# Differential attention with the query projection two heads ahead and the key projection one

## What is computed

```
q, k, v = jnp.split(h @ w_in, [2 * H * dk, 4 * H * dk], axis=-1)
q = apply_rope(...); k = apply_rope(...)        # 2 halves of 64 per head
s = jnp.einsum('bqhcd,bkhcd->bhcqk', qi, k) * scale
p = masked_softmax(s, key_pos[None, :] <= qpos[:, None])
a = p[:, :, 0] - lam * p[:, :, 1]               # the difference of two softmaxes
o = jnp.einsum('bhqk,bkhd->bqhd', a, v)
o = rms_norm(o, subln_g) * (1.0 - lambda_init)
return o.reshape(B, S, H * dv) @ w_out
```

## Time and profile before

| | us |
|---|---|
| median of 3 runs (1627.14 to 1628.72) | 1627.54 |
| the profiled execution | 1626.89 |
| its span, as the hardware profiler has it | 1625.1 |
| TensorE busy | 1511.1 (93%) |
| VectorE busy | 815.0 (50%) |
| ScalarE busy | 711.6 (44%) |
| GpSimd busy | 577.1 (36%) |

### The profile page before, as it was taken

One profiled execution on the slowest core, in us unless ns is written; L12 is line 12 of the kernel. 1 busy time (PEld: TensorE's weight loads), 2 busy tenths in 40 slices (PEclk: granted clock), 3 DMA queues, 4 the chain that ended last, 5 costly groups with the idle time before them and its releaser, 6 DMA issues. The chain is left out here.

```text
span 1625.1 us, 22951 instructions
## 1 busy us (share of the span) xinstructions
PE 1511.1 (93%) x7566; PEld 1246.5 (77%) x7566; DVE 815.0 (50%) x1233; ACT 711.6 (44%) x1245; POOL 577.1 (36%) x343
## 2 busy tenths in 40 slices
PE   6898887999999999999889898989999999999988
PEld 5766655888888888778778787878788888888877
DVE  5666665365455410155556777676364554420053
ACT  5243433454444422247436364636364444432252
POOL 3524534344454444333310101010244444444332
PEclk9988987999999999999899999999999999999999
DMA  4311010132322322232410101010133223222222
GB/s 172 122 34 53 26 52 26 66 130 90 102 91 91 102 101 94 78 119 78 158 41 14 40 14 39 13 39 13 52 117 102 92 90 103 95 99 91 91 88 81
DMA packets 35336, 125.96 MB, mean 78 GB/s; under 512 B 4304, under 2 KB 5072, under 8 KB 35024
## 3 DMA queue, kind: packets, MB, share of 16 engines
q1 hardware_dynamic: 31824, 115.88, 21.0%
q10 hardware_dynamic: 3456, 9.33, 1.6%
HBM read 123.09 MB, written 2.10 MB: 77 GB/s over the span
## 5 line engine op out<-in xcount | busy, mean ns | idle before, releaser
L291 POOL TENSOR_TENSOR w_lo<-w_raw,w_hi 128x1024 fp32r<-128x1024 f32 x213 | 528.4, 2483 | 918.6 <-ACT w_hi L360 918.5
L1173 PE MATMUL banks_a<-nT_hi,w_hi 128*128 128x512 f32 (+1 forms) x936 | 356.5, 381 | 3.3 <-DVE nT_lo L759 3.0
L360 ACT ACTIVATE w_hi<-w_raw 128x1024 fp32r<-128x1024 f32 x213 | 225.6, 1061 | 305.6 <-PE banks_b L1182 128.1
L1173 PE MATMUL banks_a<-nT_lo,w_hi 128*128 128x512 f32 (+1 forms) x936 | 354.0, 378 | 0.0
L1173 PE MATMUL banks_a<-nT_hi,w_lo 128*128 128x512 f32 (+1 forms) x936 | 353.5, 378 | 0.0
L1173 PEld LDWEIGHTS banks_a<-nT_hi,w_hi 128*128 128x128 f32 x936 | 180.3, 193 | 35.6 <-DVE nT_lo L759 3.9
L1173 PEld LDWEIGHTS banks_a<-nT_lo,w_hi 128*128 128x128 f32 x936 | 179.8, 192 | 31.0
L1173 PEld LDWEIGHTS banks_a<-nT_hi,w_lo 128*128 128x128 f32 x936 | 179.4, 192 | 31.4
L434 ACT ACTIVATE y<-banks_a,conv 128x512 f32<-128x512 f32 x88 | 68.7, 780 | 203.9 <-PE banks_a L1173 203.4
L809 DVE SCALAR_TENSOR_TENSOR y<-banks_a,conv,y 128x511 f32<-128x511 f32 x88 | 66.0, 750 | 177.8 <-ACT y L434 177.3
L908 DVE TENSOR_REDUCE nm<-banks_b 128x2 f32<-128x256 f32 (+2 forms) x96 | 79.1, 824 | 59.5 <-PE banks_b L1332 39.4
(11 more groups left out here) (260 smaller groups left out, 2613.3 us busy)
## 6 DMA issues: line engine op xcount, KB each, us to landing
w_raw<-in_w SPq DMA_DIRECT2D x213, 512.0 KB, 3.2
g_pre<-in_gains ACTq DMA_DIRECT2D x6, 512.0 KB, 3.7
x<-in_x SPq DMA_DIRECT2D x4, 512.0 KB, 9.5
g_post<-in_gains ACTq DMA_DIRECT2D x4, 512.0 KB, 5.1
out<-x SPq DMA_DIRECT2D x4, 512.0 KB, 2.7
pe_raw<-in_pT ACTq DMA_DIRECT2D x2, 512.0 KB, 4.4
w1k<-in_w ACTq DMA_DIRECT2D x1, 1024.0 KB, 4.9
w1v<-in_w ACTq DMA_DIRECT2D x1, 1024.0 KB, 6.8
```

The source lines that it names most:

```text
L291: pool.tensor_tensor(w_lo[slot][:, :], w_raw[k % RAW][:, :], w_hi[slot][:, :].bitcast(F32), ALU.subtract).then_inc(S["w_lo_done"], 1)
L360: act.activation(w_hi[u % RING][:, :], w_raw[u % RAW][:, :], ACT.Copy).then_inc(S["w_hi_done"], 1)
L1173: m = pe.matmul(bank[:, cols], w[:, k * P:(k + 1) * P], r[:, k, cols], start=(k, pas) == (0, 0), stop=(k, pas) == (KT - 1, 2))
```

## The change

The queries are now projected two heads ahead and the keys one head ahead. The weight units are used in the same order as before: keys of h + 1, then queries of h + 2.

- TensorE projects, within head h, the keys of h + 1 first (between the first scores and the second values) and then the queries of h + 2. The queries of head 1 are projected before head 0. The six parts of a head stand at the same six places as before, only part 3 and what follows hold queries; head 6 has keys only, head 7 nothing.
- VectorE ropes the keys of h + 1 between mixes 2 and 3, and does `query_half(h + 2)` at the end of the head. `o_variance` moves ahead of the third maximum, and the fourth maximum ahead of mix 2.
- ScalarE does the fourth pair of exponentials before the third `pT`, moves the first `w_high` of a head behind that `pT`, and the second behind the last `pT`. Three instead of two `w_high` of queries and keys are made before head 0.
- GpSimd does one `low`, then the query rope, then `o_normed`, then the other `low`.
- The loops cover heads 1 to 4; heads 5 to 7 are written out.

The scores themselves are the same instructions.

```diff
--- before.py
+++ after.py
@@ -331,11 +331,11 @@
             lows(0, ahead)
             with chain.loop(0, (DIFF_HEADS - 2) // 2, 2 * (4 * NEWTON + 1)) as i:
                 for p in range(2):
+                    u = ahead + 2 * p
+                    low(u, u % RING, u + 4 * i + 1)
+                    query_rope(2 * i + (p + 2), p)
                     o_normed(2 * i + p)
-                    query_rope(2 * i + (p + 2), p)
-                    for k in range(2):
-                        u = ahead + 2 * p + k
-                        low(u, u % RING, u + 4 * i + 1)
+                    low(u + 1, (u + 1) % RING, u + 4 * i + 2)
             o_normed(DIFF_HEADS - 2)
             o_normed(DIFF_HEADS - 1)
             lows(ahead + 2 * (DIFF_HEADS - 2), UNITS)
@@ -562,7 +562,8 @@
                 signal(act.activation(oT0_hi[:, bass.ds(h, 1), :].rearrange("p a n -> p (a n)"), A[2][:, :],
                                       ACT.Identity, scale=subg[:, :]), "oThi_done", h + 1)
 
-            def head(h, p, first=False, last=False, i=0, per=0, u=0):
+            def head(h, p, first=False, keys=True, queries=True, i=0, per=0, u=0):
+
                 exps(h, p, 0)
                 exps(h, p, 1)
                 if not first:
@@ -570,25 +571,26 @@
                 p_turned(h, 0)
                 exps(h, p, 2)
                 p_turned(h, 1)
-                if not last:
+                exps(h, p, 3)
+                p_turned(h, 2)
+                if keys:
                     w_high(u, i, per)
-                p_turned(h, 2)
-                exps(h, p, 3)
                 if not first:
                     oT_high(h - 1)
-                if not last:
+                p_turned(h, 3)
+                if queries:
                     w_high(u + 1, i, per)
-                p_turned(h, 3)
 
             UH = PLAN["qk"] + RING
-            w_high(UH)
-            w_high(UH + 1)
+            for u in range(3):
+                w_high(UH + u)
             act.wait_ge(S["lam_ready"], 1)
-            head(0, 0, first=True, u=UH + 2)
-            with chain.loop(0, (DIFF_HEADS - 2) // 2, 2) as i:
+            head(0, 0, first=True, u=UH + 3)
+            with chain.loop(0, (DIFF_HEADS - 4) // 2, 2) as i:
                 for p in range(2):
-                    head(2 * i + (p + 1), (p + 1) % 2, i=i, per=4, u=UH + 4 + 2 * p)
-            head(DIFF_HEADS - 1, 1, last=True)
+                    head(2 * i + (p + 1), (p + 1) % 2, i=i, per=4, u=UH + 5 + 2 * p)
+            for h in range(DIFF_HEADS - 3, DIFF_HEADS):
+                head(h, h % 2, keys=h < DIFF_HEADS - 1, queries=h < DIFF_HEADS - 2, u=UH + 3 + 2 * h)
             o_out(DIFF_HEADS - 1)
             w_high(PLAN["out0"] + RING)
             oT_high(DIFF_HEADS - 1)
@@ -955,33 +957,34 @@
                 rope(A[k], (qT, kT)[k][p][:, :], ("qrope_done", "krope_done")[k], h + 1,
                      tmp=(sh[:, :], t1[:, :], t2[:, :]), scale=(1.0, SCALE)[k])
 
-            def head(h, p, first=False, last=False):
+            def head(h, p, first=False, keys=True, queries=True):
+
                 maxima(0, 0, "scores_done", "negmax_done", 4 * h)
                 maxima(1, 2, "scores_done", "negmax_done", 4 * h + 1)
                 mix(h, p, 0)
                 mix(h, p, 1)
-                maxima(2, 0, "scores_done", "negmax_done", 4 * h + 2)
                 if not first:
                     o_variance(h - 1, 1 - p)
+                maxima(2, 0, "scores_done", "negmax_done", 4 * h + 2)
+                maxima(3, 2, "scores_done", "negmax_done", 4 * h + 3)
                 mix(h, p, 2)
-                maxima(3, 2, "scores_done", "negmax_done", 4 * h + 3)
-                if first:
-                    head_rope(h + 1, 1 - p, 0)
-                elif not last:
-                    query_half(h + 1)
+                if keys:
+                    head_rope(h + 1, 1 - p, 1)
                 mix(h, p, 3)
                 if not first:
                     oT_low(h - 1)
-                if not last:
-                    head_rope(h + 1, 1 - p, 1)
+                if queries:
+                    query_half(h + 2)
 
             head_rope(0, 0, 0)
             head_rope(0, 0, 1)
+            head_rope(1, 1, 0)
             head(0, 0, first=True)
-            with chain.loop(0, (DIFF_HEADS - 2) // 2, 2 * (12 + 3 + 1 + 5)) as i:
+            with chain.loop(0, (DIFF_HEADS - 4) // 2, 2 * (12 + 3 + 1 + 5)) as i:
                 for p in range(2):
                     head(2 * i + (p + 1), (p + 1) % 2)
-            head(DIFF_HEADS - 1, 1, last=True)
+            for h in range(DIFF_HEADS - 3, DIFF_HEADS):
+                head(h, h % 2, keys=h < DIFF_HEADS - 1, queries=h < DIFF_HEADS - 2)
             o_variance(DIFF_HEADS - 1, 1)
             oT_low(DIFF_HEADS - 1)
 
@@ -1355,29 +1358,35 @@
                     m = transpose(A[2][:, tok(t)], o_nrm[:, t, :])
                 m.then_inc(S["oT_done"], 1)
 
-            def head(h, p, first=False, last=False):
-                def proj(*parts):
-                    if not last:
+            def head(h, p, first=False, keys=True, queries=True):
+
+                def next_keys(*parts):
+                    if keys:
                         for part in parts:
-                            project(h + 1, part, 1 - p)
+                            project(h + 1, 3 + part, 1 - p)
+
+                def later_queries(*parts):
+                    if queries:
+                        for part in parts:
+                            project(h + 2, part, p)
                 pe.wait_ge(S["qrope_done"], h + 1)
                 pe.wait_ge(S["krope_done"], h + 1)
                 scores(h, p, 0)
                 scores(h, p, 1)
-                proj(0, 1)
+                next_keys(0, 1)
                 turn_mix(h, 0)
                 scores(h, p, 2)
                 values(h, 0)
                 turn_mix(h, 1)
                 scores(h, p, 3)
-                proj(2)
+                next_keys(2)
                 values(h, 1)
                 turn_mix(h, 2)
-                proj(3)
+                later_queries(0)
                 if not first:
                     pe.wait_ge(S["pT_done"], 4 * h + 3)
                     turn_o(h - 1)
-                proj(4, 5)
+                later_queries(1, 2)
                 if not first:
                     pe.wait_ge(S["oTlo_done"], h)
                 turn_mix(h, 3)
@@ -1387,12 +1396,15 @@
             pe.wait_ge(S["v_done"], 4)
             for part in range(6):
                 project(0, part, 0)
+            for part in range(3):
+                project(1, part, 1)
             pe.wait_ge(S["v_done"], 8)
             head(0, 0, first=True)
-            with pe.Fori(0, (DIFF_HEADS - 2) // 2) as i:
+            with pe.Fori(0, (DIFF_HEADS - 4) // 2) as i:
                 for p in range(2):
                     head(2 * i + (p + 1), (p + 1) % 2)
-            head(DIFF_HEADS - 1, 1, last=True)
+            for h in range(DIFF_HEADS - 3, DIFF_HEADS):
+                head(h, h % 2, keys=h < DIFF_HEADS - 1, queries=h < DIFF_HEADS - 2)
 
             def last_head(n):
                 if n == 2:
```

## The result

| | before | after |
|---|---|---|
| median, us | 1627.93 (1627.14 to 1628.72) | 1608.29 (1606.34 to 1608.79) |
| the profiled execution | 1626.89 | 1606.34 |
| its span | 1625.1 | 1604.5 |
| end of the attention's last values | 279.54 | 253.19 |

The ratio is 0.9877, 95% interval 0.986 to 0.9894: the change makes the kernel faster by 19.6 us, against 20.8 forecast. The prediction holds as a time. The profile shows that it holds partly by two misses of nearly equal size, and the experiments show that the orders that came with the change gain more by themselves than the whole of it. (Lines of the changed kernel are shifted: VectorE's L796 to L799 are L798 to L801, L921 is L923, L941 is L943; TensorE's L1152 is L1155, L1329 is L1332, L1348 is L1351.)

The account below looks back on a forecast made before the run. Attention heads were taken as bound by a chain of waits around TensorE, its falling clock the second cost. Heads 1 to 6 -18.2, head 0 -1.6, head 7 -1.0: -20.8 from 1627.54 gives 1606.7 us, range 1597 to 1620 (8 in 10).

Parts of the forecast that it names:

- (a): Chain of one attention head with the keys projected first and roped before mix 3: 2.24 us wait goes, head 21.9 us.
- (b): TensorE's own work in a head, 19.0 us, fits under the chain with about 2.9 us of waits; o_nrm wait goes.
- (c): TensorE's clock in the attention heads: one fall in two heads, costing 0.3 us a head.
- rival 1: TensorE's clock keeps falling in every head: heads come to 24 us, the kernel to 1619; chance 0.17.
- (d): Head 0, with three more parts projected ahead: starts at most 0.3 us later, takes 22.0 + 0.3 for 23.93 us.
- (e): Last two heads: head 6, without queries to project, takes 23.8 us; head 7 gains 1.0 from earlier exponentials.
- (f): Weight units and their DMAs: nothing waits, costed at nothing; up to 19 us if each of eight DMAs were late.
- Rival 2: GpSimd and VectorE miss each other in the heads, no collisions: head 19.8 us, kernel 1592; chance of the whole 0.08.
- Rivals 3 and 4: In the heads: slower through GpSimd collisions and lower clock, 1634; or the move isn't felt, 1627; chance 0.04 each.

Follow-up runs that it names:

- two heads ahead alone: The changed kernel with the orders of VectorE and ScalarE as before, queries still projected two heads ahead: 1614.08 us, ratio 0.9921.
- the swap: The kernel before with two ScalarE lines exchanged, the second w_high of a head behind the last pT: 1602.44 us, ratio 0.9852.
- both: The changed kernel with GpSimd's query rope ahead of the first w_lo and ScalarE's oT_high ahead of the first w_high: 1593.49 us, ratio 0.9794.
- rope first: The changed kernel with GpSimd's query rope ahead of the first w_lo of a head: 1599.51 us, ratio 0.9836.
- the fixed place: The changed kernel with the first MLP's loop at a fixed place in instruction memory on TensorE, VectorE and ScalarE: 1601.99 us.
- orders only: The kernel before with only the change's new orders on VectorE and ScalarE, queries still one head ahead: 1599.25 us, ratio 0.983.

## Why the prediction was right, and where it was not

**The time**: a gain of 20.8 forecast, 19.6 measured by the medians, 20.55 by the profiled executions. At the end of the attention it was 26.35, of which 5.75 went later.

**(a) The chain of a head**: right almost step by step. From the start of the head at 126.32: mixes 0 and 1 end at 6.6 (6.7 forecast), the variance at 8.2 (8.3), the exponentials of tile 2 at 10.7 (10.7), mix 2 at 12.0 (12.3), the rope at 14.9 (15.1), w_lo at 17.2 (17.5), mix 3 at 18.0 (18.9), oT_lo at 18.9 (19.7), the next head at 21.6 (21.9). Of the 0.9 us at mix 3, 0.6 are an error of addition: w_lo caught its third small step, when two of them were already done, but I counted the mix whole behind w_lo. From the end of oT_lo to the next scores it took 2.7 us for the 2.2 of the forecast: 0.25 until the last transposes start, then 2.45.

What was wrong in (a) is the reason. "The wait of 2.24 us goes", because the rope leaves the boundary, is true of the changed kernel (and of two heads ahead alone), but the rope needn't leave it. 1.96 of L798's 2.65 us were the collision with w_lo; had I asked, of the collision that I had found, which instruction releases that w_lo, and where the change puts it, the swap on ScalarE would have stood out: with it alone and the rope in its old place, the wait is 0.75 us and a head 21.6.

**(b) TensorE's own 19.0 us** was 0.5 too little: 20.17 less 0.62 of waits is 19.55 in "both", 21.61 less 0.75 and 1.36 is 19.5 in the swap. The waits under the chain were so 1.5 us and some tenths, not 2.9; the 0.7 us before the first transposes didn't come at all in heads 1 to 5. The o_nrm wait went, as said: o_nrm is written at 139.48, 13.2 us in (13.3 forecast), and asked for at 140.60.

**(c) The clock**: 0.3 us a head was forecast, none was lost; this and mix 3 make heads 1 to 5 107.5 us for 111.0. Waits of 0.70, 0.21 and 0.60 us in a head left it at 1.00. The Trainium skill (TensorE: Matmul & The Clock Gate, "A second HAM failure mode: psum-queue depth-cycling"), by which many micro-idles make the clock swing as well, isn't borne out at these sizes: rival 1, at 24 us a head, falls. The kernel with one swap has waits of 0.75 and 1.37 in a head, also at 1.00; heads with one of 2.24 to 2.40 are at 0.88 to 0.93, but for the one at 0.99 shown above.

**(d) Head 0** is the step that failed: 22.3 forecast, 23.23 measured and a start 0.86 us later, so that head 1 starts at 104.83 where it started at 104.67 (-1.6 forecast, +0.2 measured). Its first transposes wait longest, 2.29 us for the first mix; the clock is 0.93 in it. In four of the six other kernels with queries two heads ahead it lasts 21.7 to 21.8 us, in two 22.9 and 23.0, so the change is at the upper one of two values and the forecast was between them. They go with the clock: all seven kernels wait 2.29 us for that first mix, and behind it the clock stays up in the four (a mean of 1.00) and falls to the lower level in the three (0.93). What decides it wasn't tested. The late start is a second miss: 0.3 us at most had been allowed for the three parts and the rope ahead of head 0.

**(e) Heads 6 and 7**: 22.03 for the 23.8 forecast, and 3.05 us off the last head for the 1.0 forecast. In head 7 TensorE's waits for o_nrm (3.22 us) and oT_lo (2.06) before have become waits for pT (2.25, 0.63) and oT_lo (1.69) after; their sum falls by 0.6 us only. The rest is TensorE's own time, 12.02 us for 14.49 at a mean clock of 0.76 for 0.58. I had priced this head without a term for the clock, and the clock isn't the change's doing alone: with the same orders in the last head it lasts 20.4 us at 0.58 in "rope first" and 20.7 at 0.67 with the fixed place, near the 20.9 that the forecast gives.

**(f) Weights**: nothing waited, as costed.

Together: head 0 +1.8, heads 1 to 5 -3.5, head 6 -1.8, head 7 -2.05 against the forecast, -5.55 in all, and +5.75 behind the attention, which the prediction held at nothing. That the total came out is the luck of these two. Rival 2 (1592, no collisions at all) didn't come with the change, but it is what "both" comes close to: its rope and wide mix are free of GpSimd, one collision is left (L919 of the first mix, 1.44 us at 126.96, until w_lo is over at 128.38), a head takes 20.15 us for the 19.8 priced, the kernel 1593.5. Rivals 3 and 4 had no part.

## What to carry to other kernels

When an instruction on the critical chain is held up by another engine, look for what *releases* the one that holds it up: moving that release by one place (here one w_high behind one pT, 24.6 us) can be worth as much as a rebuilt schedule (19.6). Price each part of a change alone, and where two of them remove the same wait, count it once. And an idle gap behind which TensorE's clock falls costs nearly as much again as the gap (here 2.0 us beside 2.24), so the 1.5 us that the swap took from it were worth 3.4. The last head and the head before the loop show the other side: part of such a gain depends on where the clock happens to fall, so compare the granted clocks before you credit a stage's time to the change.

## What the runs showed of the hardware

- A VectorE instruction waits for a GpSimd instruction under way even if it is tiny: L919 on 128 x 1 took 1.76 us for 0.22. The instructions that were held up in the rows shown have two tensors in SBUF among their operands; one that reads PSUM ran at its usual time beside a w_lo (with orders only, L796 from 161.06 took 0.69 us, the w_lo ran from 158.67 to 161.51).
- The granted clock was 1.00 in heads with single waits of up to 1.37 us, and 0.88 to 0.93 in heads with one of 2.24 to 2.40, with one exception at 0.99; with two heads ahead alone, a head with 1.38 and 1.59 us had 0.96. Behind one and the same wait of 2.29 us in head 0 the clock stayed at 1.00 in four kernels and fell to 0.50 in three. Filling the wait of 2.24 us in each head of the kernel before with matmuls whose result isn't used made the kernel 15.6 us faster.
- The issue of one small DMA on ScalarE took 0.45 us in most kernels and 1.7 to 2.4 in four, the instructions of the stage being the same; in two pairs of kernels it was short again where a loop ahead of it stood at a fixed place. A whole stage with unchanged code differs by up to 4 us between kernels. A gain of that size in the total says little without the stage's own bounds.
